# A two-layer encoder trunk on one core: the first two chunks of a phase are run together, folds are taken two steps later, and the loops are written out

## The reference, cut to what matters

```python
for layer in range(2):
    h = rms_norm(x, mixer_norm_w[layer])
    if layer == 0:
        proj = h @ hyb_w_in                      # 2048 x 3584
        mixed = concat(attn(q, k, v), sgu(u, g)) @ hyb_w_out
    else:
        qkv = h @ sb_w_qkv                       # 2048 x 6144
        mixed = stick_breaking(q, k, v) @ sb_w_out
    x = x + mixed
    h = rms_norm(x, ffn_norm_w[layer])
    x = x + (silu(h @ w_gate) * (h @ w_up)) @ w_down   # hidden 5632
```

## Time and profile before

| | us |
|---|---|
| median of 3 runs (lowest to highest) | 2173.82 (2171.59 to 2181.28) |
| the profiled execution's own time | 2175.11 |
| its span in the trace | 2173.2 |
| PE busy | 2124.4 (98%) |
| DVE busy | 1229.8 (57%) |
| ACT busy | 983.3 (45%) |
| POOL busy | 112.6 (5%) |
| mean granted TensorE clock | 0.992 |

### The profile page before, as it was taken

The page is one execution under the profiler, slowest core; times in us unless marked ns, Lnnn a source line. Parts: engine busy times, 40 slices in busy tenths (PEclk is TensorE's granted clock), DMA queues, the critical chain, the costliest instruction groups (busy, mean ns, idle before and its releaser), DMA issues.

```text
span 2173.2 us, 25840 instructions
## 1 busy us (share of the span) xinstructions
PE 2124.4 (98%) x9436; PEld 1744.1 (80%) x9436; DVE 1229.8 (57%) x1382; ACT 983.3 (45%) x1150; POOL 112.6 (5%) x189
## 2 busy tenths in 40 slices
PE   9999999999999999988999999999999999999989
PEld 8777778888888888876788888778888888888877
DVE  6777655555555545554565565555555454645554
ACT  6566554443434434444555455454443444434343
POOL 1000100100010000001000000110000000000000
PEclk9999999999999999999999999999999999999999
DMA  9544666665566656656654554676665667655744
GB/s 330 179 137 157 222 220 213 221 219 196 193 211 200 231 194 198 207 183 202 197 169 159 173 174 161 203 225 216 211 221 199 197 213 222 213 196 196 226 155 154
DMA packets 210595, 434.31 MB, mean 200 GB/s; under 512 B 9360, under 2 KB 9376, under 8 KB 210272
## 3 DMA queue, kind: packets, MB, share of 16 engines
q1 hardware_dynamic: 197728, 392.72, 54.9%
q0 software_dynamic: 12384, 38.56, 5.9%
q10 hardware_dynamic: 416, 2.13, 0.3%
HBM read 413.45 MB, written 19.92 MB: 199 GB/s over the span
## 4 chain that ended last, share of the span: by engine, by line
PE 83%; DMA 9%; DVE 3%; issue 2%; ACT 1%; POOL 1%; DVEq 0%; ACTq 0%; SPq 0%
PE acc L1052 27%; PE acc L1053 26%; PE acc L1054 26%; DMA spread<-blocks 6%; DMA blocks<-folded 3%; POOL spread L414 1%; DVE w_lo L687 1%; DVE folded L737 1%; PE turn L1068 1%; PE turn L1132 0%; ACT xT_hi L492 0%; DVE xT_lo L748 0%; PE turn L1177 0%; ACT m_hi L490 0%; PE zb L1152 0%
## 5 line engine op out<-in xcount | busy, mean ns | idle before, releaser
L687 DVE TENSOR_TENSOR w_lo<-raw,w_hi 128x1024 fp32r<-128x1024 f32 (+1 forms) x760 | 895.4, 1198 | 544.6 <-ACT w_hi L473 543.6
L473 ACT ACTIVATE w_hi<-raw 128x1024 fp32r<-128x1024 f32 (+1 forms) x760 | 781.9, 1039 | 825.7 <-PE acc L1054 822.5
L1052 PE MATMUL acc<-w_hi,xT_hi 128*128 128x512 f32 x2016 | 793.6, 394 | 9.1 <-DVE xT_lo L748 5.0
L1054 PE MATMUL acc<-w_hi,xT_lo 128*128 128x512 f32 x2016 | 785.3, 390 | 0.0
L1053 PE MATMUL acc<-w_lo,xT_hi 128*128 128x512 f32 x2016 | 785.2, 389 | 0.0
L1052 PEld LDWEIGHTS acc<-w_hi,xT_hi 128*128 128x128 f32 x2016 | 378.8, 188 | 95.4 <-DVE w_lo L687 6.6
L1054 PEld LDWEIGHTS acc<-w_hi,xT_lo 128*128 128x128 f32 x2016 | 378.7, 188 | 79.3
L1053 PEld LDWEIGHTS acc<-w_lo,xT_hi 128*128 128x128 f32 x2016 | 378.9, 188 | 78.3 <-issue 1.7
L1052 PE MATMUL acc<-w_hi,m_hi 128*128 128x512 f32 x960 | 380.9, 397 | 33.6 <-DVE w_lo L687 19.3
L1053 PE MATMUL acc<-w_lo,m_hi 128*128 128x512 f32 x960 | 377.6, 393 | 0.0
L1054 PE MATMUL acc<-w_hi,m_lo 128*128 128x512 f32 x960 | 377.2, 393 | 0.0
(11 more groups left out here) (148 smaller groups left out, 618.5 us busy)
## 6 DMA issues: line engine op xcount, KB each, us to landing
raw<-in_w_gate SPq DMA_DIRECT2D x88, 1024.0 KB, 5.2
raw<-in_w_up SPq DMA_DIRECT2D x88, 1024.0 KB, 5.3
raw<-in_w_down SPq DMA_DIRECT2D x80, 1024.0 KB, 5.0
raw<-in_w_qkv SPq DMA_DIRECT2D x48, 1024.0 KB, 5.2
raw<-in_w_out SPq DMA_DIRECT2D x32, 1024.0 KB, 5.0
raw<-in_w_in SPq DMA_DIRECT2D x26, 1024.0 KB, 5.2
blocks<-folded POOLq DMA_DIRECT2D x34, 512.0 KB, 3.2
spread<-blocks POOLq DMA_DIRECT2D x136, 128.0 KB, 4.8
```

The costliest lines, as they stand in the source:

```text
L473: nc.scalar.activation(w_hi[:, s % RING, 0:nk, :], raw[:, u % RING, k:k + nk, :], ACTF.Copy).then_inc(hi_ready, 1)
L687: nc.vector.tensor_tensor(w_lo[:, s % RING, 0:nk, :], raw[:, (s // 2) % RING, k:k + nk, :], f32(w_hi[:, s % RING, 0:nk, :]), ALU.subtract) ...
L1052: nc.tensor.matmul(dst, h, wh, start=q == 0 and k == 0, stop=False)
L1054: ins = nc.tensor.matmul(dst, l, wh, start=False, stop=q == ph.per_chunk - 1 and k == nk - 1)
```

## The change

Units are always 4 k-tiles, also in the last down. out and down become one pass with 4 chunks. A new table (class Iteration) lists the halves of each pass. In out, in down, and in the first pass of up0 and of qkv the first two chunks are paired: all but the last four k-tiles of chunk 0, all but the last four of chunk 1, then the last four of chunk 0 and the last four of chunk 1. The other chunks follow as before.

Accumulator pairs alternate over all chunks of the kernel, also over phases; PE waits at a chunk's first half for the evacuation of the chunk two before.

A fold is taken 6 steps after it is made (FOLD_LAG) instead of 4. It is made in `between`, so behind a half on DVE, not ahead of it; for chunk 1 of a paired renewing phase two steps later still (`fold_at`). `spread` is doubled and POOL waits for a landing before it goes on to the next fold. The add goes in place into x_sb; the copy back and its semaphore go. `kT` has memory of its own. All loops are written out.

```diff
-FULL = [4] * (KT // 4)
-REST = [4, 4, 2, 2]
-FEED_FORWARD = [ph for n, part in enumerate(PARTS)
-                for ph in (("up", part, 2, FULL, n), ("down", D // CH, 1, FULL if part == 4 else REST, n))]
+FEED_FORWARD = [ph for n, part in enumerate(PARTS) for ph in (("up", part, 2, KT, n), ("down", 1, D // CH, 4 * part, n))]
 PHASES = [
-    ("in", 1, 7, FULL, 0), ("out", 4, 1, FULL, 0), *FEED_FORWARD,
-    ("qkv", 4, 3, FULL, 0), ("out", 4, 1, FULL, 0), *FEED_FORWARD,
+    ("in", 1, 7, KT, 0), ("out", 1, D // CH, KT, 0), *FEED_FORWARD,
+    ("qkv", 4, 3, KT, 0), ("out", 1, D // CH, KT, 0), *FEED_FORWARD,
 ]
+AHEAD = 2
+FOLD_LAG = 6
+class Iteration:
+    def __init__(self, ph, i, base, chunk0):
+        units = [(c, k) for c in range(ph.chunks) for k in range(0, ph.tiles, UNIT)]
+        self.paired = ph.name in ("out", "down") or ph.name in ("up", "qkv") and i == 0 and ph.part == 0
+        if self.paired:
+            late = ph.tiles - UNIT
+            units = ([(c, k) for c in range(2) for k in range(0, late, UNIT)] + [(0, late), (1, late)] + units[2 * ph.tiles // UNIT:])
...
+    def pair(self, c):
+        return (self.chunk0 + c) % 2
+    def fold_at(self, c):
+        return self.ends[c] + (2 if self.paired and c == 1 and self.ph.renews else 0)
...
+            def bounce(F):
                 pool.wait_ge(fold_done, F + 1)
                 pool.dma_start(blocks.rearrange("t p n -> p t n"), folded[:, :, :]).then_inc(fold_out, 16)
                 pool.wait_ge(fold_out, 16 * F + 16)
+                if F >= 2:
+                    pool.wait_ge(fold_lo, F - 1)
...
+                pool.wait_ge(fold_landed, 16 * QUARTERS * (F + 1))
...
-                if t == ph.slots + 2:
-                    nc.scalar.activation(x_sb[:, :, bass.ds(i * CH, CH)], fresh(ph)[:, :, :], ACTF.Copy).then_inc(kept, 1)
...
             def residual(it, t):
+                for c in range(it.ph.chunks):
+                    if t == it.fold_at(c):
+                        dve.wait_ge(x_added, 2 * (before * (D // CH) + c) + 2)
+                        fold(it.ph.fold(c), x_sb[:, :, c * CH:(c + 1) * CH])
+                    if t == it.fold_at(c) + FOLD_LAG:
+                        F = it.ph.fold(c)
+                        fold_take_lo(F, [by_tile(xT_lo[:, c * 4 + k:c * 4 + k + 1, :]) for k in range(4)],
...
-                iteration(0, True)
-                if ph.count > 1:
-                    with pe.Fori(1, ph.count) as i:
-                        iteration(i, False)
+            for it, h in HALVES:
+                for work_of in running(h.index):
+                    between(*work_of)
+                half(it, h)
```

More of the change, by code:

```diff
@@ L62 @@
 RING = 4
+UNIT = 4
 XT_PIECES = [0, 2, 4, 6, 8, 12, KT]
@@ L68, with __init__ @@
 class Phase:
-    def __init__(self, n, unit0, chunk0, turn0, up0, before, rows0, fold0):
-        self.name, self.count, self.chunks, self.unit_tiles, self.part = PHASES[n]
+    def __init__(self, n, sums, taken):
+        self.n = n
+        self.name, self.count, self.chunks, self.tiles, self.part = PHASES[n]
         self.layer = 0 if n < LAYER1 else 1
-        self.hidden0, self.up0 = sum(PARTS[:self.part]), up0
-        self.before, self.rows0 = before, rows0
+        self.hidden0 = sum(PARTS[:self.part])
+        self.adds = self.name in ("out", "down")
@@ L78, in __init__ @@
         self.renews = self.name == "out" or self.name == "down" and self.part == len(PARTS) - 1 and n < len(PHASES) - 1
[L79 to L82, removed]
+        self.before, self.rows0, self.up0, self.read0, self.turn0, self.fold0 = sums
         self.turns = {"in": 23, "qkv": 4}.get(self.name, 0)
-        self.folds, self.fold0 = int(self.name == "up" or self.renews), fold0
@@ L87, in half @@
-    def half(self, i, s):
-        return self.half0 + i * self.slots + s
+        self.folds = self.count if self.name == "up" else self.chunks if self.renews else 0
+        self.iterations = []
+        for i in range(self.count):
+            self.iterations.append(Iteration(self, i, taken[0], taken[1]))
+            taken[0] += self.iterations[-1].slots
+            taken[1] += self.chunks
     def chunk(self, i, c):
-        return self.chunk0 + i * self.chunks + c
-    def last_half(self, i, c):
-        return self.half(i, (c + 1) * self.per_chunk - 1)
+        return self.read0 + i * self.chunks + c
@@ L100, in fold, with running @@
         return self.fold0 + i
[L102 to L106, removed]
 def make_phases():
-    out, unit0, chunk0, turn0, up0, before, rows0, fold0 = [], 0, 0, 0, 0, 0, 0, 0
+    out, sums, taken = [], [0] * 6, [0, 0]
     for n in range(len(PHASES)):
-        ph = Phase(n, unit0, chunk0, turn0, up0, before, rows0, fold0)
+        ph = Phase(n, tuple(sums), taken)
         out.append(ph)
[L114 to L121, removed]
+        for k, more in enumerate((ph.adds, ph.renews, ph.count if ph.name == "up" else 0, 0 if ph.adds else ph.count * ph.chunks,
+                                  ph.count * ph.turns, ph.folds)):
+            sums[k] += int(more)
     return out
 PH = make_phases()
+ITERATIONS = [it for ph in PH for it in ph.iterations]
+HALVES = [(it, h) for it in ITERATIONS for h in it.halves]
+CHUNKS = [(it, c) for it in ITERATIONS for c in range(it.ph.chunks)]
+FOLDS = [(it, 1, it.i) if it.ph.name == "up" else (it, c, c) for it in ITERATIONS if it.ph.folds
+         for c in ([1] if it.ph.name == "up" else range(it.ph.chunks))]
+def running(g):
+    return [(it, g - it.base) for it in ITERATIONS if 0 <= g - it.base < it.slots + 16]
 BLOCKS = 2 * A_KV
 BLOCK0 = 22
-IN_END = PH[0].slots
+IN_END = PH[0].iterations[0].slots
 def block_start(n):
@@ L461, in half @@
                     ins.then_inc(xt_hi, 1)
[L462 to L473, removed]
+                if h.index in (0, 2):
+                    act.wait_ge(first_landed[h.unit], 16)
+                elif h.part == 0 or h.index in (1, 3):
+                    act.wait_ge(raw_landed[h.raw_slot], 16 * (h.unit // RING + 1))
+                if h.index >= RING:
+                    act.wait_ge(products_done, 2 * (h.index - RING) + 2)
+                nc.scalar.activation(w_hi[:, h.slot, :, :], raw[:, h.raw_slot, 2 * h.part:2 * h.part + 2, :], ACTF.Copy).then_inc(hi_ready, 1)
             def take_hi(K, dst, src, scale=None):
@@ L993, in _, with leaves @@
-            leave(PH[-1], PH[-1].count - 1, 0)
+                elif it.ph.name == "up":
+                    up_work(it, t)
+                elif it.ph.name == "qkv":
+                    qkv_work(it, t)
+                else:
+                    residual(it, t)
+            def leaves(g):
+                for it, t in running(g):
+                    for c, end in enumerate(it.ends):
+                        if t == (11 if (it.ph.n, c) == (0, 0) else end):
+                            leave(it, c)
@@ L1036, in half @@
-            def half(n, i, s, first):
-                ph = PH[n]
-                c, q = s // ph.per_chunk, s % ph.per_chunk
-                k0, nk = ph.tiles(s)
+                    pe.wait_ge(dve_took, prev.turn(h.k0 // 4, 2 + h.k0 // 2 % 2) + 1)
+                elif prev.folds:
+                    pe.wait_ge(fold_lo, prev.fold(h.k0 // 4) + 1)
+            def half(it, h):
+                ph = it.ph
                 hi, lo = lhs(ph)
-                if first and c == 0:
-                    stationary_ready(n, s)
-                pe.wait_ge(lo_ready, ph.half(i, s) + 1)
+                if it.i == 0 and h.c == 0:
+                    stationary_ready(it, h)
+                pe.wait_ge(lo_ready, h.index + 1)
@@ L1045, in half @@
                 for tt in range(TT):
[L1046 to L1054 removed]
+                    if h.opens and it.chunk0 + h.c >= 2:
+                        pe.wait_ge(*evacuated(*CHUNKS[it.chunk0 + h.c - 2], tt))
@@ new lines, in half @@
+                    dst = acc[:, it.pair(h.c), tt, :]
+                    for k in range(2):
+                        at = slice(tt * P, (tt + 1) * P)
+                        xh, xl = hi[:, h.k0 + k, at], lo[:, h.k0 + k, at]
+                        wh, wl = w_hi[:, h.slot, k, :], w_lo[:, h.slot, k, :]
+                        nc.tensor.matmul(dst, xh, wh, start=h.opens and k == 0, stop=False)
+                        nc.tensor.matmul(dst, xh, wl, start=False, stop=False)
+                        ins = nc.tensor.matmul(dst, xl, wh, start=False, stop=h.closes and k == 1)
```

415 lines of the change are left out of this document (173 added, 242 removed).

## The result

The changed kernel takes 2120.11 us (median of 4, 2118.54 to 2123.01) against 2173.0 of the kernel before (2171.59 to 2181.28): ratio 0.975, 95% interval 0.9723 to 0.9778, so 53 us faster. The forecast was 2124, from a saving of 50. The profiled execution took 2121.32 us, 53.8 less than the one of before, with a span of 2119.5.

What follows compares the result with a forecast made beforehand. PE's rate was taken as the first limit (busy 98%), with 61.0 us of losses a better order could remove; less 10.9 us of new losses, 50 us saved from 2173.8 gives 2124 us, range 2112 to 2140.

Steps and rivals of the forecast that it cites:

- its two big places: Most of the saving was to come from down2 of layer 0 (28.6 us less 5.3) and of layer 1 (10.3 us).
- up1 and up2 their stalls: In both layers, up1 and up2 were to lose their whole loss with takes at +6, 4.8 us together.
- the end of the kernel: In down2 of layer 1, some 4.1 us of the 14.4 us loss are the kernel's end.
- The stall model: Behind a take of x, w_lo is ready at T+20.7 but PE wants it at T+19.0: 1.7 us stall in out.
- hand calculation of what is late next: New stalls from queued trips and folds made behind takes, in down2, first qkv pass, out and up0; 10.9 us with clock charge.
- a fall of the clock: After down2's largest new stall PE's matmuls would run at the lower clock level; charged 1.0 us.
- the stall of 3.3 us: In down2 of layer 0, fold 3 stands behind fold 2's take, so w_lo comes at 76.7 where PE wants it at 73.4.
- The 13.4: About the mean trip through DRAM from fold to landing, in us, from nine trips; the longest was 14.4.
- Loops at 0: Writing out all loops, 43 repeated passes, was to gain 0 us, since looped down0 ran at the written-out rate.
- The 1.2 us for the w_lo: On VectorE the transposes now stand behind a w_lo, which delays the w_lo behind the take by 1.2 us, to T+21.9.
- Rival A: Trips on the one POOL lane bind, making takes in paired phases late by 2 to 5 us: 2142 us; chance 0.15.
- Rival C: The stalls left are nothing, because VectorE gets past its takes earlier: 2113 us; chance 0.09.

Runs made afterwards that it cites:

- experiment 2: The kernel before with folds taken one step later (slots+5 instead of slots+4), unpaired: 2154.7 us, ratio 0.9894.
- experiment 8: The changed kernel with folds before takes and ahead of the half, two trips at a time, and a lag of four: 2137.8 us, ratio 0.9827.
- experiment 3: The changed kernel with less lag than its six, all else kept: lag of four 2194.5 us, ratio 1.0074; lag of five 2148.7 us, ratio 0.9869.
- experiment 5: The changed kernel with the fold made before the take on VectorE where both fall on one step: 2114.9 us, ratio 0.9714.
- the repeat: The changed kernel itself, unaltered, run again as a base for some experiments: 2119.3 us, ratio 0.9738 to the kernel before.
- experiment 1: The kernel before with all its loops written out and nothing else changed: 2178.9 us, ratio 1.0016.
- experiment 9: The changed kernel with folds ahead of the half and two trips at a time, but no pairing and a lag of five: 2148.2 us, ratio 0.9882.
- experiments 6 and 7: Experiment 5's kernel with two DRAM buffers and no POOL wait for landings, 2112.94 us; then also with transposes ahead of the half, 2112.91 us.
- experiment 4: The changed kernel with no chunks paired and a lag of five instead of six: 2189.4 us, ratio 1.0049.

## Why the prediction was right, step by step

The number and its two big places were right, and for the reason given. down2 lost its waits in both layers (28.6 and 10.3 us, now 0), up1 and up2 their stalls (4.8, now 0), and the end of the kernel stayed (3.7 of 4.1).

The stall model held where the fold stands ahead of the half: 1.7 us per take before, gone with one more step (experiment 2), back with two fewer (experiment 8, 25 us of 30). With the fold behind the half it gave the direction and too small a size (experiment 3).

Its hand calculation of what is late next was right in place and mechanism. The fold made behind a take at the same step is the loss after, in the first qkv pass, in out and up0; experiment 5 moves one call and it goes. The term was mis-sized: 10.9 us against 7.2 in the profiled execution and 4.5 in that of the repeat, and experiment 5 gave back 4.4. I had charged 1.0 us for a fall of the clock; the clock stayed at 1.00, and no break in PE's work after the in phase was over 1.5 us. The rest is the stall of 3.3 us that was 1.5, because fold 2 landed 1.1 us sooner and its take was shorter. The calculation also took 13.2 and 13.0 us for its two queued trips, where 13.4 throughout would have made that stall 3.9.

The 13.4 itself came out by luck. It was read off nine trips of the kernel before; all 34 there average 12.6 us from fold to landing, the twelve of x 13.0. In the changed kernel the 29 that did not queue average 13.4 (12.5 to 15.3).

Loops at 0: right (experiment 1). The page "Runtime: NRT & Kernel Launch" of the Trainium skill, "Instruction fetch mechanics", would have the branches cost; here writing them out is worth 1.0016 (0.9994 to 1.0038), so the measurement decides against it for this kernel, whose loops on PE were among those written out. That section also says that fetch is mostly hidden in straight code, and with 1.72 times the packets that agrees: the down phases of the changed kernel took 87.1 us. What writing out did move is the trips at the start of down0 and down1 (experiment 1), which the forecast did not have.

What the forecast got only half: it treated pairing, lag and the fold's place as terms to be added. They are not. With the fold behind the half, pairing with a lag of four gave 1.0074 and a lag of five without pairing 1.0049, both a loss; with it ahead, a lag of five without pairing gave 0.9894 (experiment 2) and 0.9882 (experiment 9). That the sum came out all the same is luck in part: the change has the pairing and the lag of six together, and with both the fold's poor place costs some 6 us at most (experiments 5 to 7). The 1.2 us for the w_lo that now stands ahead of the transposes was too small for a phase's start, where VectorE is catching up: without pairing it was 2.4 (4.6 against 2.2), and the trip grew too.

Rival A, that the trips bind, fell: POOL did wait for landings, but removing this wait was worth no more than 2 us in the paired kernel (without pairing, 12). Rival C's 2113 is where experiments 6 and 7 ended, but only with further edits.

Left open: why a trip takes some 10 us in some places and 12 to 14 in most, 18 once. It runs beside the weight loads, but no run here took these away from it. That the seventh kernel is better than the sixth was not shown. The full-size units in down2, the alternating accumulators and the add in place were in every changed kernel and were not tried alone: how much of down2's gain is theirs, and not the lag's or the pairing's, is not known. All of the experiments without pairing kept 11 us or more of loss in down2 of layer 0.

## What to carry to other kernels

Where a slow round trip is taken back in an in-order queue that also feeds the bottleneck, write the times at which each item behind the take is ready and wanted; the stall is the difference, and one step of lag takes up to one step of the bottleneck off it, until it is gone, then nothing. Lag and reordering of the consumers belong together: a longer lag needs the consumer to want the data later, and without that it can deadlock. Where two pieces of side work fall on one step, the one that starts a trip goes before the one that waits for one.

## What the runs showed of the hardware

The clock after a wait of PE, read from the starts of its matmuls in six of the traces (before, changed, experiments 2, 3 and 4; a break is the distance of two starts less 0.23): behind the 17 breaks of 1.2 to 1.8 us they went on 0.23 us apart; behind 21 breaks of 1.9 to 3.3 us they went on so in nine cases and 0.43 us apart in twelve; behind all 21 breaks of 3.9 us and more they were 0.43 apart. In some cases the first two to five were still 0.23 apart and only the next ones 0.43. Here is one of 2.2 us, in up2 of the changed kernel with a lag of five, on PE:

```profile
880.50 0.39 PE L1023 MATMUL acc<-w_hi,xT_lo 128*128 128x512 f32 x1
882.90 0.50 PE L1021 MATMUL acc<-w_hi,xT_hi 128*128 128x512 f32 x1 [2.01 <-DVE w_lo L683]
```

and what followed it:

```profile
884.16 0.63 PE L1022 MATMUL acc<-w_lo,xT_hi 128*128 128x512 f32 x1
884.59 0.63 PE L1023 MATMUL acc<-w_hi,xT_lo 128*128 128x512 f32 x1
```

So a stall of 2 us can cost nearly 4. Its length alone does not tell which: the longest break that was followed by 0.23 is of 3.3 us (lag of four), the shortest followed by 0.43 of 1.9 (experiment 4). The changed kernel has no break over 1.5 us after the in phase, and its clock is 1.00.

Weight traffic of 241 GB/s with fold trips beside it did not slow PE in down2 (65.3 us for 288 matmuls, 0.2267 each).
